# Order of loads, roots and norm chunks in a two-layer diffusion trunk kernel

## The reference, cut to what matters

```python
h  = _modulate(_rms_norm(x, norm_g[0]), sh1, sc1)      # first norm; hc likewise from ctx
y, yc = _even_mixer(h, hc, ...)                        # inside: rms_norm of the queries and of the keys/values
x  = x + g1 * _rms_norm(y, norm_g[1])
h2 = _modulate(_rms_norm(x, norm_g[2]), sh2, sc2)      # second norm
x  = x + g2 * _rms_norm(ffn(h2), norm_g[3])            # ctx likewise
```

## Time and profile before

| | us |
|---|---|
| median of 3 runs | 1649.92 |
| lowest and highest | 1648.91, 1650.42 |
| profiled execution, own time | 1652.2 |
| its span | 1650.2 |
| PE busy in it | 1613.1 (98%) |
| DVE busy, ACT busy | 1127.3, 928.5 |

### The profile page before, as it was taken

How to read it: one execution, slowest core, us unless ns; L and a number is a source line. 1 busy time by engine, 2 the same in 40 slices (tenths; PEclk the granted TensorE clock), 3 DMA queues, 4 the chain that set the end, 5 groups by cost and what they waited for, 6 DMA issues and landing times.

```text
span 1650.2 us, 22626 instructions
## 1 busy us (share of the span) xinstructions
PE 1613.1 (98%) x8256; PEld 1300.7 (79%) x8256; DVE 1127.3 (68%) x1504; ACT 928.5 (56%) x1335; POOL 45.3 (3%) x66
## 2 busy tenths in 40 slices
PE   7999999999999999999999999999999999999998
PEld 3884479888888888788687888888888888888886
DVE  5442433548553333753768999899999999899998
ACT  4413433621212332642667777787778777777875
POOL 0000000300000000000101000000000000000000
PEclk9999999999999999999999999999999999999999
DMA  8523631695442222452237999999999999999982
GB/s 347 211 77 128 255 129 52 262 405 220 185 167 104 88 102 102 166 207 77 62 131 290 420 421 420 367 398 372 373 396 360 388 361 410 378 377 370 377 340 78
DMA packets 68378, 427.82 MB, mean 259 GB/s; under 512 B 8784, under 2 KB 12624, under 8 KB 20304
## 3 DMA queue, kind: packets, MB, share of 16 engines
q1 hardware_dynamic: 60000, 396.93, 62.0%
q0 software_dynamic: 8304, 29.90, 4.9%
HBM read 403.20 MB, written 23.61 MB: 259 GB/s over the span
## 4 chain that ended last, share of the span: by engine, by line
PE 92%; DVE 4%; ACT 2%; DMA 1%; issue 1%; SPq 0%; DVEq 0%; ACTq 0%
PE ps L1894 27%; PE ps L1896 27%; PE ps L1895 27%; PE ps L1912 2%; PE ps L2092 1%; PE ps L1958 1%; PE ps L2443 1%; DMA raw<-in_w 1%; PE ps L2157 1%; DVE small L1361 1%; PE ps L2136 1%; DVE raw L1551 0%; PE ps L2161 0%; PE ps L2405 0%; DVE raw L1550 0%
## 5 line engine op out<-in xcount | busy, mean ns | idle before, releaser
L1720 DVE TENSOR_TENSOR wl<-raw,wh 128x1024 fp32r<-128x1024 f32 x522 | 615.4, 1222 | 60.4 <-ACT wh L1020 53.6
L1020 ACT ACTIVATE wh<-raw 128x1024 fp32r<-128x1024 f32 x522 | 525.0, 1057 | 95.0 <-PE ps L1896 94.9
L1894 PE MATMUL ps<-wh,ah 128*128 128x512 f32 (+1 forms) x864 | 329.5, 381 | 0.5
L1896 PE MATMUL ps<-wh,al 128*128 128x512 f32 (+1 forms) x864 | 320.5, 371 | 0.0
L1895 PE MATMUL ps<-wl,ah 128*128 128x512 f32 (+1 forms) x864 | 319.8, 370 | 0.0
L1894 PE MATMUL ps<-ah,wh 128*128 128x512 f32 (+1 forms) x784 | 282.7, 361 | 4.0 <-DVE al L1149 2.6
L1896 PE MATMUL ps<-ah,wl 128*128 128x512 f32 (+1 forms) x784 | 274.8, 350 | 0.0
L1895 PE MATMUL ps<-al,wh 128*128 128x512 f32 (+1 forms) x784 | 274.4, 350 | 0.0
L1119 DVE TENSOR_TENSOR wl<-raw,wh 128x1024 fp32r<-128x1024 f32 x120 | 141.9, 1223 | 101.5 <-ACT wh L581 101.4
L1896 PEld LDWEIGHTS ps<-wh,al 128*128 128x128 f32 x864 | 162.8, 188 | 28.9
L1894 PEld LDWEIGHTS ps<-wh,ah 128*128 128x128 f32 x864 | 162.8, 188 | 28.4 <-issue 3.6
(11 more groups left out here) (285 smaller groups left out, 1565.2 us busy)
## 6 DMA issues: line engine op xcount, KB each, us to landing
raw<-in_w SPq DMA_DIRECT2D x372, 1024.0 KB, 6.7
sent<-raw POOLq DMA_DIRECT2D x16, 512.0 KB, 24.5
back<-raw POOLq DMA_DIRECT2D x16, 512.0 KB, 25.3
x<-sent POOLq DMA_DIRECT2D x7, 512.0 KB, 11.9
back<-x POOLq DMA_DIRECT2D x7, 512.0 KB, 9.0
x<-in_x SPq DMA_DIRECT2D x2, 1024.0 KB, 8.6
raw<-in_ukv SPq DMA_DIRECT2D x1, 1024.0 KB, 7.8
ah<-flat_rows POOLq DMA_DIRECT2D x2, 512.0 KB, 6.9
```

Source lines behind the costliest of these rows:

```text
L1020: act.activation(wh[:, J % SPLITS, piece_half(h)], slot(J % SLOTS)[:, piece_half(h)], ACT.Copy).then_inc(w_hi, 1)
L1720: ins = dve.tensor_tensor(wl[:, J % SPLITS, piece_half(h)], slot(J % SLOTS)[:, piece_half(h)], wh[:, J % SPLITS, piece_half(h)].bitcast(F3 ...
L1894: pe.matmul(out, lh, rh, start=start, stop=False)
L1896: return pe.matmul(out, ll, rh, start=False, stop=stop)
```

## The change

The first main piece is loaded ahead of modulation pieces 0 to 3, and its split stands earlier in both streams: on ACT ahead of the first root, on DVE ahead of the wait for that root. DVE norms four chunks instead of six ahead of the first shift and scale. ACT makes the queries' root between the queries' squares and the keys'. At the second norm DVE and ACT take four latent chunks (`LEAD`) ahead of the context's residual; ACT's output unit 7 and the context's root move behind the third and the fourth of them, and PE's remaining modulation pieces, its sum of unit 7 and the context's eight sums are spread over the first two half pieces, the columns of the modulation into the third. One filler goes.

```diff
-    return (mods(0, JOINT) + main(0, 2) + mods(JOINT, MOD_FIRST) + main(2, WIN) + ...
+    return (main(0, 1) + mods(0, JOINT) + main(1, 2) + mods(JOINT, MOD_FIRST) + main(2, WIN) + ...
-FIRST_SLOTS = (7, 8, 3, 9, 0, 1, 2, 3, 9, 2)
+FIRST_SLOTS = (0, 7, 8, 3, 9, 1, 2, 3, 9, 2)
+LEAD = 4
-           + [e for k in range(KD) for e in ((N_E2L, k), (N_EYC, k))] + each(N_E2C)
+           + each(N_E2L, LEAD) + [e for k in range(KD - LEAD) for e in ((N_EYC, k), (N_E2L, k + LEAD))]
+           + each(N_EYC)[KD - LEAD:] + each(N_E2C)
@@ scalar
             act.wait_ge(consts_set, 1)
+            split(0)
             root(N_E1)
             rows(0)
-            split(0)
...
             squares(N_Q, lambda k: zq[:, k, :], chunks=range(QR))
+            root(N_Q)
             squares(N_KV, lambda k: zkv[:, k, :], chunks=range(KVR))
-            root(N_Q)
...
             root(N_E2L)
-            out_unit(7)
-            root(N_EYC)
             for k in range(KD):
                 modulate_e2(N_E2L, k)
+                if k == 2:
+                    out_unit(7)
+                if k == 3:
+                    root(N_EYC)
+                if k >= LEAD:
+                    stream_square(N_E2C, k - LEAD)
+            rows(ATT_MODS // JOINT)
+            for k in range(KD - LEAD, KD):
                 stream_square(N_E2C, k)
-                if k == 4:
-                    rows(ATT_MODS // JOINT)
@@ vector
             ins.then_inc(sq_ready, 1)
+            split(0)
             inverse(N_E1)
             dve.wait_ge(mod_used, 2)
-            for k in range(KD - 2):
+            for k in range(4):
                 normed(N_E1, x[:, k, :], xn[:, k, :], k)
...
-            split(0)
...
-            for k in range(KD - 2, KD):
+            for k in range(4, KD):
                 normed(N_E1, x[:, k, :], xn[:, k, :], k)
...
             inverse(N_E2L)
-            for k in range(KD + 1):
-                if k < KD:
-                    normed_stream(N_E2L, k)
-                    if k == 0:
-                        inverse(N_EYC)
-                        dve.wait_ge(evac_act, evacs(("o", 7), "act"))
-                    if k >= 2:
-                        dve.wait_ge(res_done, RES_BEFORE[N_EYC] + k - 1)
-                    normed(N_EYC, y_e[:, k, TL:T], tmp[k % 2][:, TL:T], k)
+            for k in range(LEAD):
+                normed_stream(N_E2L, k)
                 if k:
                     low(N_E2L, k - 1)
-                if k < KD:
-                    residual_add(N_EYC, 0, 1, k, tmp[k % 2][:, TL:T])
+            inverse(N_EYC)
+            dve.wait_ge(evac_act, evacs(("o", 7), "act"))
+            for k in range(KD):
+                if k >= 2:
+                    dve.wait_ge(res_done, RES_BEFORE[N_EYC] + k - 1)
+                normed(N_EYC, y_e[:, k, TL:T], tmp[k % 2][:, TL:T], k)
+                if k + LEAD < KD:
+                    normed_stream(N_E2L, k + LEAD)
+                if k + LEAD <= KD:
+                    low(N_E2L, k + LEAD - 1)
+                residual_add(N_EYC, 0, 1, k, tmp[k % 2][:, TL:T])
@@ tensor
             mod_piece(ATT_MODS + 1)
-            unit_sum(7)()
-            mod_piece(ATT_MODS + 2)
...
+            first = {(1, 1): lambda: mod_piece(ATT_MODS + 2), (1, 2): unit_sum(7), (1, 3): lambda: mod_piece(ATT_MODS + 3),
+                     (1, 5): lambda: context_sums(0), (1, 6): lambda: context_sums(1), (1, 7): lambda: context_sums(2)}
+            second = {(0, 0): lambda: context_sums(3), (0, 6): lambda: context_sums(4), (1, 1): lambda: context_sums(5),
+                      (1, 4): lambda: context_sums(6), (1, 7): lambda: context_sums(7)}
+            third = {(0, 2): lambda: mod_cols(ATT_MODS // JOINT)}
...
                 claim(("gu", u))
-                if u == 0:
-                    keep_busy(8 % 4, 1)
                 half_piece(M_GU + m, (8 + u) % 4, h,
                            (lambda k: pe.wait_ge(mod_lo, MOD_BEFORE[(N_E2L, N_E2C)[h]] + k + 1)) if m == 0 else None,
-                           {(1, k): (lambda k=k: context_sum(k)) for k in range(1, KD)} if u == 0 else {})
-                if u == 0:
-                    sum_square(N_E2C, KD - 1)
+                           {0: first, 1: second, 2: third}.get(u, {}))
```

More of the change, by code:

```diff
@@ L88, in ring_order @@
     main = lambda a, b: [("main", i) for i in range(a, b)]
-    return (mods(0, JOINT) + main(0, 2) + mods(JOINT, MOD_FIRST) + main(2, WIN) + mods(MOD_FIRST, NORM_MODS) + main(M_WOUT, M_WOUT + 3)
+    return (main(0, 1) + mods(0, JOINT) + main(1, 2) + mods(JOINT, MOD_FIRST) + main(2, WIN) + mods(MOD_FIRST, NORM_MODS) + main(M_WOUT, M_WOUT + 3)
             + mods(NORM_MODS, ATT_MODS) + main(M_WOUT + 3, M_GU + 2) + mods(ATT_MODS, OUT_MODS) + main(M_GU + 2, M_GU + MADE_FIRST + 2)
@@ L2183, in _, with context_sums @@
             mod_piece(ATT_MODS + 1)
-            unit_sum(7)()
-            mod_piece(ATT_MODS + 2)
[L2187 to L2192, removed]
+            def context_sums(*chunks):
+                for k in chunks:
+                    sum_square(N_E2C, k)
+            first = {(1, 1): lambda: mod_piece(ATT_MODS + 2), (1, 2): unit_sum(7), (1, 3): lambda: mod_piece(ATT_MODS + 3),
[3 more added lines that the diff above has]
+            third = {(0, 2): lambda: mod_cols(ATT_MODS // JOINT)}
             def made_cols(n):
```

## The result

| | before | changed |
|---|---|---|
| median, us | 1650.17 (6 runs) | 1655.81 (6 runs) |
| lowest to highest | 1648.49 to 1652.41 | 1654.59 to 1659.12 |
| profiled execution, own time | 1652.2 | 1655.95 |
| its span | 1650.2 | 1654.1 |

The changed kernel is slower: ratio 1.003, 95% interval 1.002 to 1.004. That is 5.6 us by the medians, where +1.9 was forecast, and 0.8 above the upper end of the range. The two profiled executions differ by less, 3.8. The profiled execution of before was a slow one of its kernel, 2.0 above this median, and that of the changed kernel was not.

The account below looks back on a forecast made before the run. PE was taken as the bound, 92% of the chain, with all edits in the first 330 us. +0.8 + 0.0 + 1.1 = +1.9, forecast 1651.8 us on the median's scale, range 1648.0 to 1655.0.

Parts of the forecast that it names:

- First edit, +0.8: Start: fourth modulation piece lands at 24.5, fillers end later, first real matmul moves from 30.23 to 31.0; +0.8 us.
- the gain that the fillers were said to hide: Start: data for the first real matmul ready 0.3 us earlier, but PE still stands behind its fillers.
- Second edit, 0.0: Queries' norm: PE still waits for a modulation piece landing at 145.86, so the earlier root changes nothing; 0.0 us.
- its price: Queries' norm: the low clock after 1.93 us of idle PE is kept; its absence was the bound of -1.9 us.
- Third edit, +1.1: Second norm: PE idles 2.2 us before the fourth latent chunk and the context comes late; +1.1 us, clock staying up.
- the bounds -2.2 and +3.1: Second norm: -2.2 us if all PE's losses there go, +3.1 if the clock falls after the new idle time.
- the first rival of the prediction: Second norm: the clock falls in the new gap, 296.9 to 299.1, adding 1.8 us, total 1653.6; 18%.
- The third rival: Second norm: early context root, no idle PE at the fourth chunk, context chunks not missed; -2.2, total 1648.5 us; 12%.
- The condition that I named: Second norm: the -2.2 us needs a context root early enough to avoid idle PE at chunk four and missed context chunks.

Follow-up runs that it names:

- the kernel with fillers in the gap: The third edit alone plus four filler matmuls in PE's idle time ahead of the fourth latent chunk, against the kernel before: 1651.13 against 1650.40 us, ratio 1.0008.
- root and sums sooner: The third edit alone with the context's root and its last five sums both earlier, against the kernel before: 1647.45 against 1650.40 us, ratio 0.9982.
- the two experiments: On the third edit alone, against before: output unit 7, its sum and the context's root earlier, 1650.23 us, ratio 0.9995; last five context sums earlier, 1652.11 us, ratio 1.0012.

## Why the prediction was wrong, point by point

The sign of the sum was right, and so were the bound (PE, in the first 330 us) and the waits of each edit. The size was off: +1.9 forecast, 4.0 to 5.6 measured, and 1655.8 lies outside the range. The forecast also gave 74% to a difference too small to tell from none and 20% to slower, and slower is what came.

**First edit, +0.8: right in its mechanism, small in its size.** The landing (24.5 forecast, 24.65 measured) and the place behind the fillers hold, and three fillers instead of five show that PE stood behind the fillers. The low part came 0.3 earlier after x's landing in the changed kernel than in the one trace of before, as worked out, but by the means of the traces with five fillers only 0.1. So the gain that the fillers were said to hide was hardly there. The means of the starts differ by 1.1. I took one trace of before (18.25) for the kernel, and it was at the slow end of its own spread, 16.7 to 18.3. With the old order PE idled 0.6 to 2.5 ahead of the first piece and 1.0 to 1.4 ahead of the second, and in two of the eight traces the clock was up over both pieces; in each of the new order's traces with five fillers PE idled 3.8 to 5.3 us there and the clock was low for most or all of its first two pieces.

**Second edit, 0.0: right.** The edit moves nothing here that PE waits for. The clock is another matter, and I kept its price without grounds for it. The 1.93 us of idle PE are the same in all 14 traces, but the clock fell behind them in 8, and the stretch then takes 11.4 instead of 9.8. It fell in four of the seven traces with the old order and five fillers, in all four with the new order and five fillers, and in none of the three with three fillers. Whether the loads have a hand in that or it is chance is not shown.

**Third edit, +1.1: the step that failed.** It was "I take +1.1", the choice among the bounds -2.2 and +3.1 by a sum in which the clock stays up. The gap was placed to 0.1 us, and the text itself set its rival, the fall of the clock, at 18%. In all four traces that hold an unfilled gap of 2.14 or 2.15 us there, the clock fell behind it, and in none of the other ten. The sum without the clock came out at 1.63 instead of 1.1 (in the kernel with fillers in the gap the last low part of the context was ready 35.7 behind piece 24, where 35.5 was worked out, and the fourth half piece ended 0.6 later than worked out, which I put down to small hops between its parts), and the clock added 1.0, where the rival had 1.8. Together 2.65. So the first rival of the prediction is what happened, and 0.8 + 2.65 would have given 1653.4; with 1.1 for the start, 1653.7. Both are inside the range that was given, so these two steps explain 1.85 us of the miss and not all of it.

**The third rival** (the head start counts in full) was right about what the chunks are worth and wrong about this kernel. With root and sums sooner the stretch gains 2.0 us on before, close to the -2.2 of its price. The condition that I named, no idle time at the fourth chunk and no late context, is what the two experiments supplied, and the first of them alone gained 1.1 of the 2.0.

**What stays open.** The stretches account for 1.1 + 0.0 + 2.65 = 3.75 us, the medians show 4.8 and 5.6. Both intervals (2.5 to 5.4, and 3.3 to 6.6) hold 3.75, and the tail alone runs from 1311.6 to 1315.5 from one execution to the next, so no further cause is needed; none is excluded either. The granted clock of the timed executions says where to look. Its mean is 0.9940, 0.9943 and 0.9938 in the three sets of the kernel before (101 executions), and 0.9922 and 0.9927 for the first edit alone, 0.9922 and 0.9924 for the changed kernel. Within the sets of before, 0.001 of this clock goes with 0.9 to 1.1 us of time. So the first edit's 2.5 and 2.1 us go with a clock that is lower by 0.0018 and 0.0011, about 1 to 2 us of them, while its start, the later landing included, shows 1.1 in all. More frequent falls at the queries' norm, as counted above, would fit; they are not shown to be the cause.

Nor is it shown that the fall in the new gap is certain. PE idles 2.15 or 2.16 us at about 804 us in every trace, in code that no edit touches, and the clock fell behind that gap in 8 of the 14. Before, and then the changed kernel:

```profile
804.64 0.78 PE L2125 MATMUL ps<-cst,raw 128*128 128x128 f32 x4 [2.16 <-DVE raw L1551]
...
805.00:808.40 3.40, 3.40 (x11) 1.25 (x9) 2.91 (x5) 1.93 (x5) 0.00 (x0) 0.50 0.00 0
```

```profile
809.30 0.63 PE L2133 MATMUL ps<-cst,raw 128*128 128x128 f32 x4 [2.16 <-DVE raw L1559]
...
809.30:812.70 3.40, 2.61 (x14) 1.41 (x16) 3.33 (x5) 1.93 (x5) 0.00 (x0) 1.00 0.00 0
```

## What to carry to other kernels

When an edit lets one stream run ahead of another, look for the first item of the leading stream that now stands behind a wait for the other: four chunks ahead were worth 2 us only once the other stream's root was asked for two chunks earlier, with what leads to it, and its sums came sooner. Fillers that hold the clock are part of the program order, so data that come sooner, or a filler's own start that comes later, need their number reset. And an idle stretch of TensorE is to be priced with a likely fall of the clock behind it in the forecast itself, where a like stretch of the same trace already shows one. Last, one trace of before is a poor base for a difference of 1 to 3 us: its start alone ran from 16.7 to 18.3.

## What the runs showed of the hardware that was not expected

The clock's low stretches differ from one execution to the next: with the same program up to there, the queries' norm took 9.8 to 10.0 us or 11.4, and the same gap of 2.15 us at 804 us had a fall behind it or none. With 1.88 of the 2.14 idle us filled with matmuls of no use the stretch was 1.0 us shorter, though the work behind them started at the same time. And one trace of the old order had the clock at 1.00 from x's landing to the first product and reached its first product in 16.68 us, 1.6 sooner than the one on which the prediction rests.
